# Turning the cross-attention probabilities and the gated mix by transposing DMAs in a one-core hybrid decoder layer

## The chip, the cores and the metric

One core of a Trainium2 chip runs the whole layer. The metric is the device time of one execution in microseconds.

## The reference

One decoder layer over 4096 tokens of width 1024, x <- x + W_out(concat(branch * silu(gate))), all in float32. One input projection of RMSNorm(x) feeds three groups of branches:

```python
proj = rmsnorm(x, norm_g) @ w_in          # 1024 -> 3072
# 8 heads x 64: stick-breaking attention (causal, QK-norm)
sb_out = stick_breaking_attention(q, k, v)
# 4 blocks x 64: width-4 causal convolution, then a gated linear recurrence
lru_out = rg_lru(causal_depthwise_conv(lru_x), ...)
# 4 heads x 64: cross-attention into 256 memory tokens
p = softmax(rmsnorm(xq) @ rmsnorm(mk).T * 64 ** -0.5)
xa_out = p @ mv
y = concat([sb_out * silu(g1), lru_out * silu(g2), xa_out * silu(g3)])
return x + y @ w_out
```

## The kernel before

The 4096 tokens are 32 tiles of 128. Every engine runs the same software pipeline by hand: `body(n, p)` (p is n mod 2) works on tile n in stage A (input projection), tile n-1 in stage B (the branches), tile n-2 in stage C (output projection), and prepares x of tile n+1 in stage X. `steps` runs n = -1 to 1 unrolled, n = 2 to 29 in a loop of 14 pairs, and n = 30 to 33 unrolled. Each engine's program order is fixed by hand; `have(engine, signal, tile)` makes an engine wait until a semaphore says that a step was done for that tile. Every DMA of the loop is issued from SP's queue, in program order; a wait on SP holds back all that is behind it.

Precise products are made of two f16 halves, high and low: x_hi, x_lo for the input, y_hi, y_lo for the mix, `turned[:, 0]` and `turned[:, 1]` for attention weights. `pair_product` (L1285) does hi*hi, hi*lo, lo*hi for 8 blocks of 128 rows, 24 matmuls of 512 columns into one PSUM bank. There are six for the input projection (`project(0)` to `project(5)`) and two for the output.

**TensorE's order in one `body`** (L1293 to L1470): transposes of q, k, cross-attention q and the recurrence's input of tile n-1 (L1309, L1334); project 0; stick-breaking scores (L1350); project 1, project 2; cross-attention scores (L1368) and recurrence gates (L1377); eight f32 transposes of the gated mix `xy` of tile n-2 into the two TURN banks (L1388); project 3; eight transposes of the stick-breaking weights `take` (L1406) into the same banks; project 4; weights times values (L1430, bank HEADS); project 5; a small product that spreads the row scales of the next x (L1412); eight f32 transposes of the cross-attention probabilities `probs` (L1397, in `turn_weights`), again into TURN; output product 0 of tile n-2; probabilities times memory values (L1460 to L1462) and two transposes of the recurrence's result (L1465), which signal `mixed`; output product 1 of tile n-2.

**ACT and DVE around them.** Whatever TensorE turned is taken out of PSUM in halves: ACT writes the high half in f16 (L592 in `turned_high`, L671 for the mix), DVE the low half as value minus high half (L928 in `turned_low`, L1056 for the mix), two instructions of 512 elements each. ACT writes `probs` by exp (L686), the gate sigmoid (L717), the values' high half (L730), x_hi (L738). DVE gates the branches into `xy` (L1138 to L1141), takes the row maximum (L1150), reduces it to a power of two (L1153 to L1159), scales `xy` by it (L1161), and adds the output products to the residual (L1131, L1164). Its first step of the next `body` is the evacuation of the turned q (L956).

**SP's order in one `body`** (L388 to L430): load x for the residual (L394); keep q, k and the attention carry in DRAM (L386); load x for tile n+1 (L405, after the transposes L1388, since they read `xy`) and its turned copy (L407); keep the gate and the values (L386), two copies of the values between partitions (L424, L425); store the output (L428) and wait until it has landed.

`squares`, a scratch for sums of squares, lies on `turned[:, 0]`. `spare` holds weights at the start, later x_res and the recurrence's state; its first 2048 columns are unused in the loop.

Of the kernel before, what the change touches and what calls it, by code (L numbers as in the profile page):

```python
# [27 lines left out]
F16 = mybir.dt.float16  # L28
# [8 lines left out]
P = 128  # L37
# [11 lines left out]
def hybrid_layer(nc, x, x_turned, mem, w_in_g, w_out_g, w_kv_v, per_partition, gate_blocks, out):  # L49
# [35 lines left out]
    with ctx:  # L85
# [11 lines left out]
        def few(n):  # L97
# [46 lines left out]
        mv_raw = [rec_g[:, :, :].rearrange("p h t -> p (h t)"), in_g[:, :, :].rearrange("p h t -> p (h t)")]  # L144
        h_sb = spare[:, KD * GC - D - LW:KD * GC - D].rearrange("p (h t) -> p h t", t=P)
# [49 lines left out]
        y_inv = few(1)  # L195
        y_un = sb("y_un", [P, 2, OC])
# [27 lines left out]
            gate_x gate_l gate_sb xa_scores mx_done neg_done p_done turned_p p_act p_dve  # L224
            conv gates_done gates_read tanh_done beta_steps ui_done beta_done u_done h_done
            mixed rden_done gx_done y_mixed y_steps y_scaled turned_y y_hi_done y_lo_done
# [5 lines left out]

        x_loaded = sem("x_loaded")
# [62 lines left out]
        def have_dma(eng, signal, tile):  # L296

            have(eng, signal, tile, 16)

# [59 lines left out]
        def _(sp):  # L359
# [27 lines left out]

            def body(n, p):  # L388
                X, A, B, C = stages(n)
                q = 1 - p  # L390
                if C:
                    if isinstance(n, int) and n == 2:
                        sp.wait_ge(w_lo, CH)
                    sp.dma_start(x_res, x_t[n - 2]).then_inc(res_loaded, 16)  # L394
                if B:
                    have_dma(sp, kept["q"], n - 2)
                    have_dma(sp, kept["k"], n - 2)
                    keep("q", q_kept, q_t[:, :, :], n - 1, [s["q_evac"]])
                    keep("k", k_kept, k_t[:, q, :, HALF:], n - 1, [s["k_evac"]])
                    have_dma(sp, kept["carry"], n - 2)  # L400
                    keep("carry", carry_kept, carry[:, q, :], n - 1, [s["w"]])
                if X and not (isinstance(n, int) and n < 0):
                    have(sp, s["turned_y"], n - 2)
                    have(sp, s["x_sq"], n)
                    sp.dma_start(xy[:, :], x_t[n + 1]).then_inc(x_loaded, 16)  # L405
                    have(sp, s["x_lo_done"], n)
                    sp.dma_start(x_t32[:, :, :], x_turned[n + 1]).then_inc(xt_loaded, 16)  # L407
                if isinstance(n, int) and n == 0:
                    for c in range(4, CH):
                        load_chunk(c)  # L410
                    sp.wait_ge(seen_made, 1)
                    sp.dma_start(seen[HALF:P, :], seen[0:HALF, :]).then_inc(seen_copied, 16)
                    sp.dma_start(restart[HALF:P, :], restart[0:HALF, :]).then_inc(restart_copied, 16)
                if A:
                    have_dma(sp, kept["gate"], n - 1)
                    have_dma(sp, kept["v"], n - 1)
                    keep("gate", gate_kept, gate[:, p, 0:GC], n, [s["gate_sb"]])
                    keep("v", v_kept, v_sb[:, p, :, :], n, [s["v_read"]])
                    if isinstance(n, int) and n == 0:
                        sp.wait_ge(fail_ones, 1)  # L420
                    have(sp, s["heads"], n - 1)
                    have_dma(sp, v_back_old, n - 1)
                    have_dma(sp, v_back_new, n - 1)
                    sp.dma_start(v_back[HALF:P, p, :, :], v_sb[0:HALF, p, :, :]).then_inc(v_back_old, 16)  # L424
                    sp.dma_start(v_back[0:HALF, q, :, :], v_sb[HALF:P, p, :, :]).then_inc(v_back_new, 16)  # L425
                if C:
                    have(sp, s["out_ready"], n - 2)
                    sp.dma_start(out_t[n - 2], x_res).then_inc(stored, 16)  # L428
                    have_dma(sp, stored, n - 2)
# [109 lines left out]
        def _(act):  # L539
# [56 lines left out]
            def body(n, p):  # L596
# [71 lines left out]
                if C:  # L668
                    have(act, s["turned_y"], n - 2)
                    for b in range(2):  # L670
                        last = act.activation(y_hi[:, 4 * b:4 * b + 4, :], TURN[b][:, :].rearrange("p (k t) -> p k t", t=P),  # L671
                                              ACT.Copy)
                    last.then_inc(s["y_hi_done"], 1)
                if B:
                    have(act, s["gates_read"], n - 1)
                    if isinstance(n, int) and n == 1:
                        act.wait_ge(lam_done, 1)
                    for h in range(LH):
                        act.activation(tanh_l[:, h, :], rec_g[:, h, :], ACT.Tanh, scale=rate[:, h:h + 1])
                        last = act.activation(decay[:, h, :], rec_g[:, h, :], ACT.Exp, scale=rate[:, h:h + 1])  # L680
                    last.then_inc(s["tanh_done"], 1)

                    have(act, s["neg_done"], n - 1)
                    have(act, s["rden_done"], n - 2)
                    for h in range(HX):
                        last = act.activation(probs[:, h, :], SCORE[h % 2][:, (h // 2) * NM:(h // 2 + 1) * NM], ACT.Exp,  # L686
                                              bias=neg_mx[:, h:h + 1], scale=ZSCALE, accum_out=den[:, h:h + 1])
                    last.then_inc(s["p_done"], 1)
# [32 lines left out]
                if isinstance(n, int) and n == 1:  # L721
                    chunk_high(7)
                if A:
# [7 lines left out]
                if B:  # L731
                    have(act, s["turned_p"], n - 1)
                    turned_high(s["p_act"])
                if X:
                    have(act, s["x_scaled"], n + 1)
                    if A:
                        have(act, proj_done[5], n)
                    act.activation(x_hi[:, :, :], x_t32[:, :, :], ACT.Copy).then_inc(s["x_hi_done"], 1)  # L738
                if first:
                    chunk_high(6)  # L740
# [31 lines left out]
        def _(dve):  # L772
# [160 lines left out]
            def body(n, p):  # L933
# [119 lines left out]
                if C:  # L1053
                    have(dve, s["y_hi_done"], n - 2)
                    for b in range(2):
                        last = dve.tensor_tensor(y_lo[:, 4 * b:4 * b + 4, :], TURN[b][:, :].rearrange("p (k t) -> p k t", t=P),  # L1056
                                                 y_hi[:, 4 * b:4 * b + 4, :], ALU.subtract)
                    last.then_inc(s["y_lo_done"], 1)
# [46 lines left out]
                if B:  # L1105
# [5 lines left out]
                                             ALU.mult, ALU.mult).then_inc(s["gx_done"], 1)  # L1111
                if A:
# [3 lines left out]
                if B:  # L1116
                    have(dve, s["p_act"], n - 1)
                    turned_low(s["p_dve"])
# [28 lines left out]
                if B:  # L1147
# [13 lines left out]
                    dve.tensor_scalar(xy[:, :], xy[:, :], y_inv[:, :], TOP, ALU.mult, ALU.mult).then_inc(s["y_scaled"], 1)  # L1161
                if C:
                    have(dve, out_done[1], n - 2)
                    dve.scalar_tensor_tensor(x_res[:, GC:D], PROJ[1][:, :], y_un[:, p, 1:2], x_res[:, GC:D],  # L1164
                                             ALU.mult, ALU.add).then_inc(s["out_ready"], 1)

# [77 lines left out]
        def _(pe):  # L1244
# [48 lines left out]
            def body(n, p):  # L1293
# [25 lines left out]
                if B:  # L1319
# [5 lines left out]
                    have(pe, s["p_act"], n - 2)  # L1325
                    have(pe, s["p_dve"], n - 2)
# [52 lines left out]
                if C:  # L1379
                    have(pe, s["y_scaled"], n - 2)  # L1380
                    if B:
                        have(pe, s["q_evac"], n - 1)
                        have(pe, s["k_evac"], n - 1)
                    else:
                        have(pe, s["p_act"], n - 2)
                        have(pe, s["p_dve"], n - 2)
                    for k in range(KD):
                        last = pe.transpose(TURN[k // 4][:, (k % 4) * P:(k % 4 + 1) * P], xy[:, k * P:(k + 1) * P], ident[:, :])  # L1388
                    last.then_inc(s["turned_y"], 1)
# [4 lines left out]
                def turn_weights(src, signal):  # L1394

                    for i in range(8):
                        last = pe.transpose(TURN[i // 4][:, (i % 4) * P:(i % 4 + 1) * P],  # L1397
                                            src[:, i // 2, (i % 2) * P:(i % 2 + 1) * P], ident[:, :])
                    last.then_inc(signal, 1)

                if B:
                    have(pe, s["w"], n - 1)
                    if C:
                        have(pe, s["y_lo_done"], n - 2)
# [34 lines left out]
                if B:  # L1439
                    have(pe, s["p_done"], n - 1)  # L1440
                    turn_weights(probs, s["turned_p"])
                if C:
                    have(pe, s["y_hi_done"], n - 2)
                    have(pe, s["y_lo_done"], n - 2)
# [3 lines left out]
                if B:  # L1448
                    have(pe, s["p_act"], n - 1)
                    have(pe, s["p_dve"], n - 1)  # L1450
# [111 lines left out]
```

## Time and profile before

| | us |
|---|---|
| median of 3 runs | 1756.45 (1755.13 to 1756.46) |
| the profiled execution: time | 1755.22 |
| the profiled execution: span | 1753.5 |
| TensorE busy in the span | 1672.4 (95%) |
| DVE, ACT, POOL busy | 1062.6, 824.5, 238.3 |

The span runs from the first to the last instruction. A matmul's own duration overlaps that of the next, so two things are read for TensorE: the chain of waits, which gives each group the time that it adds, and idle time before a group. A timeline row is start, busy time, engine, line, operation, output tile <- input tiles, shape, count, and in brackets the idle time before it with what ended it. PE is TensorE, PEld its weight load, SPq the SP queue's issuing instructions. DMA rows give the time from issue until the data has landed. Buffer names are those of the memory's owner: `fail_and_take` holds `take`, `probs` and `v_back`; `spare` holds x_res; `bank` is any PSUM bank.

### The profile page before, as it was taken

What the parts mean: (1) busy time and instruction counts of PE and PEld (TensorE: products, weight loads), DVE (VectorE), ACT (ScalarE), POOL (GpSimd) and SP (SyncE); (2) the same over time, 40 slices, a digit from 0 to 9 for tenths busy, and PEclk for the clock granted to TensorE, in tenths of its full rate; (3) what the DMA queues carried; (4) which work ended last, traced back from release to release, by engine and by line L of the source; (5) the groups of instructions that cost most, each with busy time, mean ns of one, the idle gap of its engine ahead of it and who ended that gap; (6) DMA issues with size and microseconds to landing.
All of it is one profiled execution on the core that took longest, in us unless ns stands there. A gap on an engine that the chain in (4) does not pass through costs nothing.

```text
span 1753.5 us, 29956 instructions
## 1 busy us (share of the span) xinstructions
PE 1672.4 (95%) x11334; PEld 892.9 (51%) x11334; DVE 1062.6 (61%) x2012; ACT 824.5 (47%) x1583; POOL 238.3 (14%) x245
## 2 busy tenths in 40 slices
PE   3886999999999999999999999999999999999986
PEld 1443555555555555555555555555555555555553
DVE  5875655655665565566556556655665665566563
ACT  5844454434545443354554335455433445543441
POOL 0110111110111111011111101111110111111010
PEclk9987999999999999999999999999999999999998
DMA  9411121221211122121112212121221212122111
GB/s 368 146 55 43 54 68 66 72 77 55 78 54 66 66 72 78 54 78 54 66 66 72 78 54 78 54 66 66 72 78 54 78 54 66 66 72 79 55 55 37
DMA packets 61215, 130.03 MB, mean 74 GB/s; under 512 B 10176, under 2 KB 26880, under 8 KB 60032
## 3 DMA queue, kind: packets, MB, share of 16 engines
q1 hardware_dynamic: 60896, 129.49, 21.6%
q8 instruction: 18, 0.29, 0.1%
q10 hardware_dynamic: 288, 0.13, 0.0%
q14 instruction: 13, 0.11, 0.0%
HBM read 70.60 MB, written 50.53 MB: 69 GB/s over the span
## 4 chain that ended last, share of the span: by engine, by line
PE 88%; issue 5%; DVE 3%; ACT 2%; DMA 1%; POOL 1%; POOLq 0%; DVEq 0%; ACTq 0%
PE bank L1288 24%; PE bank L1289 24%; PE bank L1290 24%; PE bank L1309 2%; PE bank L1377 2%; PE bank L1350 2%; PE bank L1368 2%; PE bank L1430 2%; PE bank L1406 2%; PE bank L1397 2%; PE bank L1388 1%; DVE w_pair L859 1%; DMA ident<-ident_flat 1%; PE bank L1412 0%; PE bank L1465 0%
## 5 line engine op out<-in xcount | busy, mean ns | idle before, releaser
L1288 PE MATMUL bank<-w_pair,x_hi 128*128 128x512 f16 x1536 | 587.0, 382 | 5.0 <-DVE w_pair L859 5.0
L1289 PE MATMUL bank<-w_pair,x_hi 128*128 128x512 f16 x1536 | 585.7, 381 | 0.0
L1290 PE MATMUL bank<-w_pair,x_lo 128*128 128x512 f16 x1536 | 585.4, 381 | 0.0
L1290 PEld LDWEIGHTS bank<-w_pair,x_lo 128*128 128x128 f16 x1536 | 151.1, 98 | 184.0 <-issue 4.8
L1288 PEld LDWEIGHTS bank<-w_pair,x_hi 128*128 128x128 f16 x1536 | 151.0, 98 | 176.3 <-issue 14.5
L1289 PEld LDWEIGHTS bank<-w_pair,x_hi 128*128 128x128 f16 x1536 | 151.2, 98 | 165.6 <-issue 3.6
L982 DVE TENSOR_REDUCE ss<-turned 128x8 f32<-128x512 f32 (+1 forms) x96 | 57.4, 598 | 260.2 <-ACT turned L638 172.6
L1288 PE MATMUL bank<-wo_pair,y_hi 128*128 128x512 f16 x512 | 195.3, 381 | 2.6 <-DVE y_lo L1056 2.6
L1289 PE MATMUL bank<-wo_pair,y_hi 128*128 128x512 f16 x512 | 194.9, 381 | 0.0
L1290 PE MATMUL bank<-wo_pair,y_lo 128*128 128x512 f16 x512 | 194.8, 380 | 0.0
L494 POOL TENSOR_TENSOR fail_and_take<-fail_and_take,seen 128x512 f32<-128x512 f32 x32 | 40.5, 1265 | 819.7 <-ACT fail_and_take L631 819.7
L611 ACT ACTIVATE k_t<-bank,given 128x256 f32<-128x256 f32 x32 | 15.1, 473 | 251.5 <-PE bank L1334 251.5
L1017 DVE SCALAR_TENSOR_TENSOR gate<-bank,unscale,gate 128x256 f32<-128x256 f32 (+1 forms) x96 | 54.7, 570 | 118.5 <-ACT gate L717 75.7
L503 POOL TENSOR_TENSOR rs<-rs,columns 128x20 f32<-128x20 f32 x32 | 113.0, 3533 | 5.5 <-POOL rs L501 5.1
L928 DVE SCALAR_TENSOR_TENSOR turned<-bank,turned 128x512 f16<-128x512 f32 x128 | 82.5, 686 | 46.6 <-ACT turned L592 46.6
L616 ACT ACTIVATE q_raw<-bank,unscale 128x512 f32<-128x512 f32 x32 | 22.0, 686 | 128.4 <-PE bank L1290 128.4
L730 ACT ACTIVATE v_sb<-bank 128x512 f16<-128x512 f32 x32 | 19.1, 597 | 134.1 <-PE bank L1290 134.1
L1290 PEld LDWEIGHTS bank<-wo_pair,y_lo 128*128 128x128 f16 x512 | 50.3, 98 | 61.2 <-issue 1.4
L592 ACT ACTIVATE turned<-bank 128x512 f16<-128x512 f32 x128 | 69.1, 594 | 24.6 <-PE bank L1397 24.5
L1288 PEld LDWEIGHTS bank<-wo_pair,y_hi 128*128 128x128 f16 x512 | 50.3, 98 | 56.3 <-issue 3.6
L1289 PEld LDWEIGHTS bank<-wo_pair,y_hi 128*128 128x128 f16 x512 | 50.3, 98 | 54.2 <-issue 0.8
L992 DVE TENSOR_TENSOR_SCAN fail_and_take<-fail_and_take,restart 128x516 f32<-128x516 f32 x64 | 75.1, 1215 | 1.5 <-POOL fail_and_take L494 1.5
(214 smaller groups left out, 2569.1 us busy)
## 6 DMA issues: line engine op xcount, KB each, us to landing
xy<-in_x SPq DMA_DIRECT2D x32, 512.0 KB, 3.3
x_t<-in_x_turned SPq DMA_DIRECT2D x32, 512.0 KB, 4.1
spare<-in_x SPq DMA_DIRECT2D x32, 512.0 KB, 3.8
out<-spare SPq DMA_DIRECT2D x32, 512.0 KB, 2.6
wo_pair<-in_w_in SPq DMA_DIRECT2D x4, 2048.0 KB, 10.1
gate_kept<-gate SPq DMA_DIRECT2D x32, 256.0 KB, 2.0
v_kept<-v_sb SPq DMA_DIRECT2D x32, 256.0 KB, 2.0
fail_and_take<-v_sb SPq DMA_DIRECT2D x64, 128.0 KB, 2.3
```

Of the source, the lines that this page charges most:

```text
L494: pool.tensor_tensor(take[:, :, HALF:], take[:, :, HALF:], seen[:, :].unsqueeze(1).to_broadcast([P, HS, HALF]), ALU.mult).then_inc(s["mask ...
L503: pool.tensor_tensor(rs[:, :], rs[:, :], mhalf_c[:, :].to_broadcast([P, 20]), ALU.pow).then_inc(s["rs_done"], 1)
L592: last = act.activation(turned[:, 0, 4 * b:4 * b + 4, :], TURN[b][:, :].rearrange("p (c t) -> p c t", t=P), ACT.Copy, scale=WTOP)
L928: last = dve.scalar_tensor_tensor(turned[:, 1, 4 * b:4 * b + 4, :], TURN[b][:, :].rearrange("p (c t) -> p c t", t=P), WTOP, turned[:, 0, 4 ...
L982: dve.tensor_reduce(ss[:, at:at + heads], squares[:, 0:heads * HD].rearrange("p (h d) -> p h d", d=HD), AX.X, ALU.add).then_inc(done, 1)
L992: last = dve.tensor_tensor_scan(flat, flat, restart[:, ::-1], 1.0, ALU.mult, ALU.max)
L1017: dve.scalar_tensor_tensor(gate[:, p, cols], src, unscale[:, group:group + 1], gate[:, p, cols], ALU.mult, ALU.mult).then_inc(done, 1)
L1288: pe.matmul(dst, hi[:, k, :], pair[:, 0, k, :], start=k == 0, stop=False)
L1289: pe.matmul(dst, hi[:, k, :], pair[:, 1, k, :], start=False, stop=False)
L1290: last = pe.matmul(dst, lo[:, k, :], pair[:, 0, k, :], start=False, stop=k == KD - 1)
L1309: pe.transpose(dst, src, ident[:, :])
L1350: last = pe.matmul(SCORE[odd][top:top + HALF, c * HW:(c + 1) * HW], q_t[r, c, top:top + HALF], k_t[r, q, c, top:top + HW], start=True, sto ...
```

## The change

Both splits move ahead of the transposes. ACT makes the high half of `probs` (times 2^14) and of `xy` (times its row factor) in f16 in the rows where they lie, in `spare`; DVE makes the low halves. SP then issues four DMAs an iteration with `transpose=True`, each 128 partitions by 1024 f16 elements: two into `turned`, two into `y_hi` and `y_lo`. TensorE's 16 f32 transposes, the evacuations from PSUM and DVE's scaling of `xy` go. TensorE waits for the DMAs instead (`have_turned` is `have` with 32 counts a tile, the 16 of each of two DMAs). The turns of the mix stand first in SP's `body`, those of the probabilities between keeping the gate and keeping the values. Loading x for tile n+1 waits for the low half instead of L1388. ACT now ends its `body` with the mix's high half, DVE with its low half.

```diff
+        p_halves = spare[:, 0:D].bitcast(F16).rearrange("p (a c) -> p a c", a=2)
+        y_halves = spare[:, D:2 * D].bitcast(F16).rearrange("p (a c) -> p a c", a=2)
...
@@ sync @@
+            def turn(dst, src, signal):
+
+                sp.dma_start(dst[:, :, :], src, transpose=True).then_inc(signal, 16)
+
             def body(n, p):
...
                 if C:
+                    have(sp, s["y_low"], n - 2)
+                    have(sp, out_done[1], n - 3)
+                    turn(y_hi, y_halves[:, 0, :], y_turned)
+                    turn(y_lo, y_halves[:, 1, :], y_turned)
...
-                    have(sp, s["turned_y"], n - 2)
+                    have(sp, s["y_low"], n - 2)
                     have(sp, s["x_sq"], n)
                     sp.dma_start(xy[:, :], x_t[n + 1]).then_inc(x_loaded, 16)
...
                 if A:
                     have_dma(sp, kept["gate"], n - 1)
+                    keep("gate", gate_kept, gate[:, p, 0:GC], n, [s["gate_sb"]])
+                if B:
+                    have(sp, s["heads"], n - 1)
+                    have(sp, s["p_low"], n - 1)
+                    turn(turned[:, 0], p_halves[:, 0, :], p_turned)
+                    turn(turned[:, 1], p_halves[:, 1, :], p_turned)
+                if A:
                     have_dma(sp, kept["v"], n - 1)
-                    keep("gate", gate_kept, gate[:, p, 0:GC], n, [s["gate_sb"]])
                     keep("v", v_kept, v_sb[:, p, :, :], n, [s["v_read"]])
@@ scalar @@
-                if C:
-                    have(act, s["turned_y"], n - 2)
-                    for b in range(2):
-                        last = act.activation(y_hi[:, 4 * b:4 * b + 4, :], TURN[b][:, :].rearrange("p (k t) -> p k t", t=P),
-                                              ACT.Copy)
-                    last.then_inc(s["y_hi_done"], 1)
-                if B:
                     have(act, s["gates_read"], n - 1)
...
+                    have(act, s["p_low"], n - 2)
                     for h in range(HX):
                         last = act.activation(probs[:, h, :], SCORE[h % 2][:, (h // 2) * NM:(h // 2 + 1) * NM], ACT.Exp,
...
+                if B:
+                    have(act, s["p_done"], n - 1)
+                    have_turned(act, p_turned, n - 2)
+                    act.activation(p_halves[:, 0, :], probs[:, :, :].rearrange("p h m -> p (h m)"), ACT.Copy, scale=WTOP
+                                   ).then_inc(s["p_high"], 1)
                 if A:
                     have(act, proj_done[5], n)
...
-                if B:
-                    have(act, s["turned_p"], n - 1)
-                    turned_high(s["p_act"])
                 if X:
...
                     act.activation(x_hi[:, :, :], x_t32[:, :, :], ACT.Copy).then_inc(s["x_hi_done"], 1)
+                if B:
+                    have(act, s["y_factor"], n - 1)
+                    have_turned(act, y_turned, n - 2)
+                    act.activation(y_halves[:, 0, :], xy[:, :], ACT.Copy, scale=y_top[:, :]).then_inc(s["y_high"], 1)
@@ vector @@
-                if C:
-                    have(dve, s["y_hi_done"], n - 2)
-                    for b in range(2):
-                        last = dve.tensor_tensor(y_lo[:, 4 * b:4 * b + 4, :], TURN[b][:, :].rearrange("p (k t) -> p k t", t=P),
-                                                 y_hi[:, 4 * b:4 * b + 4, :], ALU.subtract)
-                    last.then_inc(s["y_lo_done"], 1)
...
                                              ALU.mult, ALU.mult).then_inc(s["gx_done"], 1)
+                    have(dve, s["p_high"], n - 1)
+                    dve.scalar_tensor_tensor(p_halves[:, 1, :], probs[:, :, :].rearrange("p h m -> p (h m)"), WTOP,
+                                             p_halves[:, 0, :], ALU.mult, ALU.subtract).then_inc(s["p_low"], 1)
...
-                if B:
-                    have(dve, s["p_act"], n - 1)
-                    turned_low(s["p_dve"])
...
-                    dve.tensor_scalar(xy[:, :], xy[:, :], y_inv[:, :], TOP, ALU.mult, ALU.mult).then_inc(s["y_scaled"], 1)
+                    have(dve, s["y_high"], n - 2)
+                    dve.tensor_scalar(y_top[:, :], y_inv[:, :], TOP, None, ALU.mult).then_inc(s["y_factor"], 1)
                 if C:
                     have(dve, out_done[1], n - 2)
...
+                if B:
+                    have(dve, s["y_high"], n - 1)
+                    have(dve, s["y_factor"], n - 1)
+                    dve.scalar_tensor_tensor(y_halves[:, 1, :], xy[:, :], y_top[:, :], y_halves[:, 0, :],
+                                             ALU.mult, ALU.subtract).then_inc(s["y_low"], 1)
@@ tensor @@
-                if C:
-                    have(pe, s["y_scaled"], n - 2)
...
-                    for k in range(KD):
-                        last = pe.transpose(TURN[k // 4][:, (k % 4) * P:(k % 4 + 1) * P], xy[:, k * P:(k + 1) * P], ident[:, :])
-                    last.then_inc(s["turned_y"], 1)
...
-                if B:
-                    have(pe, s["p_done"], n - 1)
-                    turn_weights(probs, s["turned_p"])
                 if C:
-                    have(pe, s["y_hi_done"], n - 2)
-                    have(pe, s["y_lo_done"], n - 2)
+                    have_turned(pe, y_turned, n - 2)
                     if A:
                         have(pe, s["gate_sb"], n)
                     pair_product(PROJ[0][:, :], y_hi, y_lo, wo_pair[:, 0], out_done[0])
                 if B:
-                    have(pe, s["p_act"], n - 1)
-                    have(pe, s["p_dve"], n - 1)
+                    have_turned(pe, p_turned, n - 1)
                     have(pe, s["gates_read"], n - 1)
```

## Rows read from the trace of the kernel before

**Rows 1.** The page: busy time of each engine, and the chain by engine.
```profile
PE 1672.4 (95%) x11334; PEld 892.9 (51%) x11334; DVE 1062.6 (61%) x2012; ACT 824.5 (47%) x1583; POOL 238.3 (14%) x245
...
PE 88%; issue 5%; DVE 3%; ACT 2%; DMA 1%; POOL 1%; POOLq 0%; DVEq 0%; ACTq 0%
```

**Rows 2.** The chain of one loop iteration: start us, us of the chain, what.
```profile
798.41 0.87 PE bank L1388 x8
...
810.71 0.95 PE bank L1430 x48
...
817.17 0.87 PE bank L1397 x8
...
835.84 1.03 PE bank L1350 x32
...
849.50 0.87 PE bank L1388 x8
```

**Rows 3.** Timeline of PE, same iteration: start us, us busy, line, tiles.
```profile
823.06 0.19 PE L1460 MATMUL bank<-mv_pair,turned 128*128 128x64 f16 x1
```

**Rows 4.** Timeline of ACT, same iteration; in brackets the idle time before.
```profile
799.47 1.10 ACT L671 ACTIVATE y_hi<-bank 128x512 f16<-128x512 f32 x2
800.42 0.44 ACT L679 ACTIVATE tanh_l<-rec_g,columns 128x128 f32<-128x128 f32 x1
...
808.02 1.07 ACT L592 ACTIVATE turned<-bank 128x512 f16<-128x512 f32 x2
...
812.14 0.69 ACT L717 ACTIVATE gate<-bank,unscale 128x512 f32<-128x512 f32 x1
```

**Rows 5.** Timeline of DVE, same iteration.
```profile
809.13 1.29 DVE L928 SCALAR_TENSOR_TENSOR turned<-bank,turned 128x512 f16<-128x512 f32 x2 [0.49 <-ACT turned L592]
...
814.68 0.48 DVE L1110 SCALAR_TENSOR_TENSOR gate<-gate,columns 128x256 f32<-128x256 f32 x1
...
829.39 0.75 DVE L1164 SCALAR_TENSOR_TENSOR spare<-bank,y_un,spare 128x512 f32<-128x512 f32 x1 [0.70 <-PE bank L1290]
830.79 0.75 DVE L956 TENSOR_SCALAR q_t<-bank,given 128x512 f32<-128x512 f32 x1 [0.65 <-PE bank L1334]
```

**Rows 6.** DVE and ACT groups by form: count | busy us, mean ns | idle before.
```profile
L1123 DVE TENSOR_TENSOR x_lo<-x_t,x_hi 128x1024 f16<-128x1024 f32 x32 | 39.2, 1225 | 35.0 <-ACT x_hi L738 35.0
...
L738 ACT ACTIVATE x_hi<-x_t 128x1024 f16<-128x1024 f32 x32 | 33.8, 1056 | 84.2 <-DVE x_t L1010 84.2
```

**Rows 7.** DMA issues: KB each, median us from issue to landing.
```profile
gate_kept<-gate SPq DMA_DIRECT2D x32, 256.0 KB, 2.0
...
fail_and_take<-v_sb SPq DMA_DIRECT2D x64, 128.0 KB, 2.3
...
k_kept<-k_t SPq DMA_DIRECT2D x32, 256.0 KB, 4.1
...
restart<-restart SPq DMA_DIRECT2D x1, 64.5 KB, 7.6
```

**Rows 8.** Timeline of the SP queue, same iteration: the issuing instructions.
```profile
819.85 0.58 SPq L425 DMA_DIRECT2D fail_and_take<-v_sb  x1
830.30 0.34 SPq L428 DMA_DIRECT2D out<-spare  x1
```

**Rows 9.** Windows: busy us of each engine, granted clock, DMA share, GB/s.
```profile
129.00:160.00 31.00, 18.79 (x145) 10.63 (x142) 18.09 (x29) 18.80 (x30) 2.84 (x5) 0.79 0.13 43
...
236.00:1696.00 1460.00, 1454.57 (x10074) 776.12 (x10073) 882.07 (x1629) 679.98 (x1347) 205.98 (x200) 1.00 0.20 66
```

**Rows 10.** The chain in iteration 1.
```profile
153.31 1.72 PE bank L1397 x8
```

**Rows 11.** The drain: DVE timeline, then PE timeline, then SP timeline.
```profile
1731.40 0.75 DVE L1164 SCALAR_TENSOR_TENSOR spare<-bank,y_un,spare 128x512 f32<-128x512 f32 x1 [1.02 <-PE bank L1290]
...
1734.83 0.59 PE L1288 MATMUL bank<-wo_pair,y_hi 128*128 128x512 f16 x1 [2.59 <-DVE y_lo L1056]
...
1734.81 0.34 SPq L394 DMA_DIRECT2D spare<-in_x  x1
```

More of the change, by code:

```diff
@@ L195, in hybrid_layer @@
         y_inv = few(1)
+        y_top = few(1)
         y_un = sb("y_un", [P, 2, OC])
@@ L223, in hybrid_layer @@
             q_read k_read xa_read lru_read sg_read v_hi v_read q_sum k_sum xq_sum rs_mid rs_done normed
-            gate_x gate_l gate_sb xa_scores mx_done neg_done p_done turned_p p_act p_dve
+            gate_x gate_l gate_sb xa_scores mx_done neg_done p_done p_high p_low
             conv gates_done gates_read tanh_done beta_steps ui_done beta_done u_done h_done
-            mixed rden_done gx_done y_mixed y_steps y_scaled turned_y y_hi_done y_lo_done
+            mixed rden_done gx_done y_mixed y_steps y_factor y_high y_low
             x_sq x_rs_mid x_rs x_diag x_wide x_scaled x_hi_done x_lo_done out_ready left_done
@@ L231, in hybrid_layer @@
         out_done = [sem(f"out_done{c}") for c in range(OC)]
+        p_turned = sem("p_turned")
+        y_turned = sem("y_turned")
         x_loaded = sem("x_loaded")
@@ L298, in have_dma, with have_turned @@
             have(eng, signal, tile, 16)
+        def have_turned(eng, signal, tile):
+            have(eng, signal, tile, 32)
         def stages(n):
@@ L722, in body @@
                     chunk_high(7)
+                    act.wait_ge(w_lo, CH)
+                if B:
[3 more added lines that the diff above has]
+                                   ).then_inc(s["p_high"], 1)
                 if A:
@@ L1324, in body @@
                     have(pe, s["y_mixed"], n - 2)
-                    have(pe, s["p_act"], n - 2)
-                    have(pe, s["p_dve"], n - 2)
                     for c in range(4):
@@ L1378, in body @@
                     last.then_inc(s["gates_done"], 1)
-                if C:
-                    have(pe, s["y_scaled"], n - 2)
-                    if B:
[L1382 to L1386, printed above, removed]
-                    for k in range(KD):
-                        last = pe.transpose(TURN[k // 4][:, (k % 4) * P:(k % 4 + 1) * P], xy[:, k * P:(k + 1) * P], ident[:, :])
-                    last.then_inc(s["turned_y"], 1)
                 project(3, [(s["k_read"], n)])
@@ L1393, in body @@
                     chunk_wide(5)
[L1394 to L1399, printed above, removed]
                 if B:
                     have(pe, s["w"], n - 1)
-                    if C:
-                        have(pe, s["y_lo_done"], n - 2)
                     for h in range(HS):
@@ L1438, in body @@
                     memory_keys_turn()
-                if B:
-                    have(pe, s["p_done"], n - 1)
-                    turn_weights(probs, s["turned_p"])
                 if C:
-                    have(pe, s["y_hi_done"], n - 2)
-                    have(pe, s["y_lo_done"], n - 2)
+                    have_turned(pe, y_turned, n - 2)
                     if A:
```

## The prediction

> **What bounds the kernel now.** I read four views in this order: the busy times and the chain by engine, the windows, the chain of one loop iteration, and the timelines of that iteration. TensorE is busy for 95% of the span and holds 88% of the chain [rows 1]. From 236 to 1696 us it is busy for 1454.57 of 1460 us at a granted clock of 1.00 [rows 9]: the loop has no hole in TensorE worth naming. The eight transposes of the gated mix (L1388) start at 798.41 in the chain and again at 849.50 [rows 2], so one iteration takes 51.09 us, and what counts in it is TensorE's own work. DVE and ACT are busy for 882.07 and 679.98 us of the same stretch [rows 9]; they matter only where something on TensorE waits for one of their results.
>
> I take the iteration from 798 to 850 us as the pattern. Its sum is against the profiled execution, 1755.22 us around a span of 1753.5; the median of the runs is 1756.45, 1.2 us above, and I carry the difference over to the median. About 0.2% (3.5 us) is what a measurement can tell from no change.
>
> **Transposes removed.** Both groups of eight lie whole on the chain: 0.87 us for L1388 and 0.87 us for L1397 [rows 2]. That is 1.74 us an iteration. It holds in iterations 2 to 31, 30 of them: 30 x 1.74 = 52.2 us, if nothing takes their place. The period would then be 49.35 us.
>
> **Do the other chains follow?** The next thing on TensorE is the product of the weights with the values (L1430). It starts at 810.71 [rows 2], and the low halves that it needs end on DVE at 809.13 + 1.29 = 810.42 [rows 5]. So it is already tight, and TensorE arriving 0.87 us earlier would gain nothing if DVE did not come earlier too. It does: ACT, which feeds DVE there, loses the evacuation L671, which starts at 799.47, at the head of ACT's unbroken run up to L592 at 808.02; the step behind it starts at 800.42 [rows 4], so without it everything there moves up by 0.95 us. Cost 0; cover gone, it would be 0.87 us an iteration (a rival below).
>
> **The split of the probabilities.** Exact new durations are not in the trace; the nearest forms are 1024 elements from SBUF to f16, 1056 ns on ACT and 1225 ns on DVE [rows 6]. They replace pairs of 512 from PSUM, about 1.07 and 1.29 us [rows 4, 5], so neither engine gets more work, and DVE also loses a scaling of 1024 elements. Bounds: 0.2 us less to 0.5 us more each; no effect on the sum while the slack below holds. ACT: the gate sigmoid ends at 812.14 + 0.69 = 812.83 [rows 4], less 0.95 is 811.9, and the new high half ends at 812.95. DVE: the gating L1110 ends at 815.16 [rows 5], less 0.95 is 814.2, so the low half lasts until about 815.45. The high half is 1.3 us ahead and makes no wait. Behind the low half on DVE stand the value split and the scaling of the next x; they come up to 1.2 us later, but DVE no longer waits there for a second evacuation (1.29), so they are about level.
>
> **The transposing DMAs of the probabilities.** SP waits for the weighted values (done at about 811.7 less 0.9) and for the low half, 815.45. From the end of a DVE result to SP's issue is 830.30 - 830.14 = 0.16 us [rows 5, 8]. One issue occupies SP for up to 0.58 us [rows 8]. A plain DMA lands 2.0 to 4.1 us after its issue for 256 KB, which is this size, and in 2.3 us for 128 KB from SBUF to SBUF [rows 7]. How long a transposing one takes the trace does not show. Low bound: as a plain one, 815.6 + 0.35 + 2.0 = 818.0. Value taken: the second issued 0.6 us after the first, landing by the slow row of 4.1: 815.6 + 0.6 + 4.1 = 820.3. High bound: the copy of a small mask from SBUF to SBUF in 7.6 us [rows 7], though behind the loads of the start, taken one after the other: 815.6 + 15.2 = 830.8. I take the value near the plain rows because a loop transfer of the same size and queue is a nearer neighbour than one copy from the crowded start. TensorE wants the turned halves when it starts L1460, at 823.06 [rows 3] less 1.74 = 821.3. **The slack is 1.0 us by the value taken**, 3.3 by the low bound, and minus 9.5 by the high one. Break-even is where the wait eats 1.74 us: both turns landed 7.6 us after the low half. Order on SP: keeping the gate now stands ahead of the turns (gate ready at 813), keeping and moving the values behind them; those are wanted an iteration later.
>
> The Trainium skill (DMA: Bandwidth & Descriptors, "Latency and other measured facts") gives a transposing DMA 261 GB/s with a non-contiguous middle dimension. By that each 256 KB takes 1.0 us on top of a fixed part, the turns would be landed by about 820, and the forecast would be the same. The same skill has a rule that speaks against the change, told with the rival.
>
> **The transposing DMAs of the mix.** Their splits are at the end of an iteration and TensorE reads them after the middle of the next. The DVE step ahead, L1164, ends at 830.14 [rows 5]; the low half adds 1.2 us to DVE before q's evacuation, L956 at 830.79 [rows 5], which then comes some 0.7 us late against TensorE's faster pace. Who waits: the scores, L1350, at 835.84 [rows 2]; L956 ends 4.3 us before that. Cost 0. SP first waits for the stored output, then issues two turns at about 834, against a use at 817.17 + 51: over 30 us of cover. They stand ahead of reloading x for the output and of keeping q and k, all with an iteration's slack. Loading the next x no longer waits for L1388, so it comes earlier. POOL's queue is not touched. Cost 0, and nothing even at the high bound.
>
> **Start and drain.** In iteration 1 the eight transposes take 1.72 us [rows 10] at a lower clock (mean 0.79 from 129 to 160 us [rows 9]), inside a chain of ACT and DVE steps; I give 1 us back, between 0 and 3. In the last iteration but one, transposes and an evacuation disappear from a loose chain: 2 us back, 0 to 4. In the last one nothing covers the mix: before, the product starts 1734.83 after y_lo [rows 11]. After, DVE's L1164, at 1731.40 + 0.75 [rows 11], comes first, then SP stores and waits until that has landed (its next issue is at 1734.81 [rows 11]), and only then turns: 0.6 + 4.1 more gives 1739.5, 4.7 us later than before. With the plain low bound it is 2.3, with the high one 15. I take 5. Start and drain together: 1 + 2 - 5 = -2.
>
> **Sum.** 52.2 - 2 = 50 us less: 1756.45 - 50 = 1706.
>
> **Rivals.**
> *A, the turned probabilities come too late (slower).* Place: TensorE before L1460, every iteration. For it: the price of a transposing DMA is not in the trace, there are two in a row, the slack is 1.0 us, and nothing else can be done by TensorE while it waits. Against: all rows of this size and queue in the loop. Price by the high bound: 9.5 us of wait. After a wait of that kind TensorE also runs slower for a while: in iteration 1, behind waits, eight transposes take 1.72 instead of 0.87 us [rows 2, 10]; say 2 us more in all. 31 x (9.5 + 2 - 1.74) = +303, and -2 - 10 of start and drain as above: about 2070. It decides from a landing 7.6 us behind the low half. The Trainium skill (VectorE: DVE Perf Modes, "The three transpose paths") has 1309 ns for one 128x128 block by DMA. By that rule, if the eight blocks of a turn do not overlap, one turn is 10.5 us and two are 21, an estimate worse than the high bound; no run here shows it. Chance 0.22 for everything beyond break-even.
> *B, the same wait, but short.* The turns land between 5.9 and 7.6 us behind the low half, and the wait eats part of the gain: with 0.9 us a time, 1706 + 28 = 1734. Chance 0.12, of which 0.02 within 0.2%.
> *C, the weights' chain does not follow.* L1430 waits for DVE as before because ACT is held by something else, and 0.87 us an iteration is lost: 1706 + 27 = 1733. Against: the run on ACT has no gap that a removed L671 would not close. Chance 0.05.
> That the change does not do what it says is not open: both groups of transposes leave TensorE's program, and nothing else of it does.
>
> **How the numbers follow.** Forecast 0.61, A 0.22, B 0.12, C 0.05. Faster: 0.61 + 0.10 + 0.05 = 0.76, same 0.02, slower 0.22. Range of the likeliest case alone: 1698 (start and drain give 5 us back, no cost at the end, a few more tenths an iteration because the value product's tightness loosens) to 1715. To hold 0.8 it must take in C and B up to a wait of 1.3 us: 1698 to 1748. What is left out is A.
>
> **What the changed profile would show.** Right: L1388 and L1397 are gone from TensorE's rows, the iteration takes 49.3 us, the granted clock stays 1.00 from 236 us on, no idle time ahead of L1460's successor, and transposing DMAs land within 4 us. Wrong: an idle time before the product of the probabilities in each iteration with a DMA as releaser (A or B, by its length), or before the value product with DVE as releaser (C). SP's instructions themselves taking microseconds would point to the issue rather than the movement as the cause of A.

## The result and the profile after

The changed kernel takes 1707.41 us (median of 4 runs, 1707.14 to 1708.2) against 1755.79 us for the kernel before on the same chip: ratio 0.9726, 95% interval 0.9709 to 0.9742. That is 48.4 us less; 50 were forecast. The profiled execution has a span of 1705.8 us.

The page of the changed kernel, busy times, DMA and the chain by engine:

```profile
PE 1617.3 (95%) x10822; PEld 836.1 (49%) x10822; DVE 1037.3 (61%) x1948; ACT 828.6 (49%) x1519; POOL 238.1 (14%) x245
...
DMA packets 196382, 163.58 MB, mean 96 GB/s; under 512 B 145344, under 2 KB 162048, under 8 KB 195200
...
q1 hardware_dynamic: 196064, 163.06, 33.3%
...
PE 89%; issue 4%; DVE 2%; ACT 1%; POOL 1%; DMA 0%; SPq 0%; POOLq 0%; ACTq 0%; DVEq 0%
```

TensorE has 512 matmuls fewer (32 tiles by 16 transposes) and is busy 55.1 us less [rows 1]; its share of the span is the same. DVE is busy 25.3 us less, ACT 4.1 us more. The DMA engines carry 33.55 MB more (163.58 against 130.03) in 135,000 more packets, all of them under 512 B, and still stand idle for two thirds of the time.

The chain of one iteration (start us, us of the chain, what); L1414 spreads the row scales of x, L1462 turns the recurrence's result, L1432 is the weights times the values (L1430 before), L1312 a matmul of the projections or of the output:

```profile
794.94 0.22 PE bank L1414 x2
...
801.04 0.25 PE bank L1462 x2
...
837.85 0.24 issue
838.10 0.95 PE bank L1432 x48
839.04 0.32 PE bank L1312
844.33 0.22 PE bank L1414 x2
```

From L1414 to L1414 it is 49.39 us, 1.70 less than the 51.09 of before [rows 2]. Thirty of them make 51.0 us. By the medians, then, start and drain took back 2.6 us, where 2 were forecast. The line "issue" ahead of L1432 is a wait: DVE's low half of the weights ends at 836.50 + 1.29 = 837.79, TensorE is ready at 837.85 and starts at 838.10.

```profile
836.50 1.29 DVE L952 SCALAR_TENSOR_TENSOR turned<-bank,turned 128x512 f16<-128x512 f32 x2 [0.49 <-ACT turned L615]
```

The chain of the kernel before has the same wait at 810.52, 0.19 us. It grew by 0.05 us, about what the loop lacks of the 1.74 of the transposes.

Now the path that could have spoiled it: the DVE timeline, PE's product of the probabilities, and the SP queue. They show two neighbouring iterations: the PE row belongs to the turns at 794.39, the DVE row to the one at 843.77.

```profile
842.45 1.21 DVE L1131 SCALAR_TENSOR_TENSOR spare<-fail_and_take,spare 128x1024 f16<-128x1024 f32 x1
```
```profile
800.18 0.19 PE L1457 MATMUL bank<-mv_pair,turned 128*128 128x64 f16 x1
```
```profile
794.39 2.65 SPq L399 DMA_TRANSPOSE turned<-spare  x2
...
810.28 1.25 SPq L399 DMA_TRANSPOSE y_hi<-spare  x1
811.57 1.33 SPq L399 DMA_TRANSPOSE y_lo<-spare  x1
813.12 0.41 SPq L411 DMA_DIRECT2D spare<-in_x  x1
...
826.44 0.35 SPq L424 DMA_DIRECT2D x_t<-in_x_turned  x1
...
843.77 1.27 SPq L399 DMA_TRANSPOSE turned<-spare  x1
```

DVE's low half ends at 843.66 and SP issues 0.11 us later. One turn holds SP for 1.3 us, against 0.34 to 0.58 for the plain DMAs of [rows 8] (0.64 is the longest plain one of this stretch, the keeping of k). The times to landing are in the DMA view:

```profile
turned<-spare SPq DMA_TRANSPOSE x64, 3.2
...
y_hi<-spare SPq DMA_TRANSPOSE x32, 3.2
y_lo<-spare SPq DMA_TRANSPOSE x32, 3.1
```

The second turn of the pair at 794.39 is issued at 794.39 + 1.34 = 795.73 and lands at 798.93; TensorE comes for it at 800.18. The slack is 1.25 us.

The drain, PE and then SP; before, the same product came after 2.59 us of waiting [rows 11]:

```profile
1686.06 0.61 PE L1312 MATMUL bank<-wo_pair,y_hi 128*128 128x512 f16 x1 [7.92 <-DMA y_lo<-spare]
```
```profile
1678.96 0.34 SPq L451 DMA_DIRECT2D out<-spare  x1
1681.59 1.23 SPq L399 DMA_TRANSPOSE y_hi<-spare  x1
1682.86 1.33 SPq L399 DMA_TRANSPOSE y_lo<-spare  x1
```

### The profile page after: what moved, and what is told of

It is laid out like the page before. It is cut to its first block, busy times and chain, and to the rows that moved or that the text cites. A ratio compares the mean times of both kernels' runs of the same rounds, so it can differ in the third digit from the quotient of the medians.

```text
span 1705.8 us, 29126 instructions
## 1 busy us (share of the span) xinstructions
PE 1617.3 (95%) x10822; PEld 836.1 (49%) x10822; DVE 1037.3 (61%) x1948; ACT 828.6 (49%) x1519; POOL 238.1 (14%) x245
## 2 busy tenths in 40 slices
DMA packets 196382, 163.58 MB, mean 96 GB/s; under 512 B 145344, under 2 KB 162048, under 8 KB 195200
## 4 chain that ended last, share of the span: by engine, by line
PE 89%; issue 4%; DVE 2%; ACT 1%; POOL 1%; DMA 0%; SPq 0%; POOLq 0%; ACTq 0%; DVEq 0%
PE bank L1312 25%; PE bank L1313 25%; PE bank L1314 25%; PE bank L1333 2%; PE bank L1399 2%; PE bank L1390 2%; PE bank L1372 2%; PE bank L1432 2%; PE bank L1408 2%; DVE w_pair L883 1%; PE bank L1462 0%; PE bank L1457 0%; PE bank L1459 0%; PE bank L1458 0%; PE bank L1356 0%
## 5 line engine op out<-in xcount | busy, mean ns | idle before, releaser
L1312 PE MATMUL bank<-w_pair,x_hi 128*128 128x512 f16 x1536 | 587.0, 382 | 5.0 <-DVE w_pair L883 5.0
L1312 PEld LDWEIGHTS bank<-w_pair,x_hi 128*128 128x128 f16 x1536 | 151.2, 98 | 176.5 <-issue 14.5
L1312 PE MATMUL bank<-wo_pair,y_hi 128*128 128x512 f16 x512 | 196.0, 383 | 7.9 <-DMA y_lo<-spare 7.9
L762 ACT ACTIVATE spare<-xy,columns 128x1024 f16<-128x1024 f32 x32 | 36.7, 1147 | 214.2 <-DVE columns L1180 214.2
L1080 DVE TENSOR_TENSOR q_raw<-q_raw,rs 128x512 f32<-128x512 f32 x32 | 37.5, 1173 | 73.2 <-POOL rs L526 73.2
L1312 PEld LDWEIGHTS bank<-wo_pair,y_hi 128*128 128x128 f16 x512 | 50.5, 99 | 62.5 <-DMA y_lo<-spare 8.4
L672 ACT ACTIVATE xq_raw<-bank,unscale 128x256 f32<-128x256 f32 x32 | 15.1, 472 | 121.3 <-PE bank L1314 121.3
```

The lines of the kernel that those rows point to most:

```text
L762: act.activation(y_halves[:, 0, :], xy[:, :], ACT.Copy, scale=y_top[:, :]).then_inc(s["y_high"], 1)
L1080: last = dve.tensor_tensor(raw[:, :, :], raw[:, :, :], rs[:, at:at + heads].unsqueeze(2).to_broadcast([P, heads, HD]), ALU.mult)
L1312: pe.matmul(dst, hi[:, k, :], pair[:, 0, k, :], start=k == 0, stop=False)
```

## The experiments

All ratios are against the kernel before, measured beside each.

**One half of the change alone, twice.** In the first kernel only the mix is split and turned by DMA, in the second only the probabilities. Each is the diff above without the other's lines; on TensorE:

```diff
 e1_mix_only: L1388 goes, L1397 stays
-                        last = pe.transpose(TURN[k // 4][:, (k % 4) * P:(k % 4 + 1) * P], xy[:, k * P:(k + 1) * P], ident[:, :])
+                    have_turned(pe, y_turned, n - 2)
 e2_probs_only: L1397 goes, L1388 stays
-                    turn_weights(probs, s["turned_p"])
+                    have_turned(pe, p_turned, n - 1)
```

> Only the gated mix is split where it lies and turned by DMA; the probabilities go through TensorE as before. My theory (the gain is TensorE's own time for the transposes, 0.87 us a group and iteration, and the DMAs are hidden): 30 x 0.87 = 26 us gained, the drain gives back about 5 (the wait for the DMA in the last iteration, 7.9 us after the change against 2.6 before), so about 1734 us (1730 to 1738), and an iteration of 50.2 us. Rival (the gain comes from lighter ACT and DVE chains or from the earlier load of x, which both belong to the mix): nearly the whole gain is here, about 1710.

> Only the probabilities are split where they lie and turned by DMA; the mix goes through TensorE as before. My theory: 30 x 0.87 = 26 us gained and 1 to 2 in the drain, so about 1728 us (1724 to 1732), if the slack of 1.2 us ahead of the product of the probabilities holds here too; the gate sigmoid on ACT comes 0.95 us later than with both changes while TensorE comes 0.87 us later, so it should. Rival (the gain belongs to the mix): about 1750 or no change.

Measured: the mix alone 1734.7 us, ratio 0.988 (0.9864 to 0.9897); the probabilities alone 1729.4 us, ratio 0.9846 (0.9829 to 0.9862). The gains are 20.4 and 25.6 us, together 46.0, against 48.4 for both at once. The chain of each, mix first, from one product with the values to the next:

```profile
800.24 0.95 PE bank L1430 x48
...
850.52 0.95 PE bank L1430 x48
...
856.97 0.87 PE bank L1399 x8
```
```profile
801.20 0.95 PE bank L1439 x48
...
851.42 0.95 PE bank L1439 x48
```

The first takes 50.28 us, 0.81 less than before; the probabilities' transposes (L1399) are still in its chain. The second takes 50.22 us, 0.87 less. The halves are alike in the loop; the mix alone has the exposed turn of the last iteration. The rival, that the gain belongs to one part's lighter chains, falls.

**The transposes back, without use.**

```diff
+                    for k in range(KD):
+                        pe.transpose(TURN[k // 4][:, (k % 4) * P:(k % 4 + 1) * P], ones[:, :], ident[:, :])
```

once ahead of project 3 and once ahead of output product 0.

> The changed kernel with both groups of eight f32 transposes put back on TensorE at their old places, on a constant, with results that nobody reads; ACT, DVE, SP and the DMAs stay as changed. My theory: TensorE's time alone decides, so about 1707 + 31 x 1.74 = 1761 us (1757 to 1764), at or above the kernel before. Rival (relief of ACT and DVE, earlier loads): part of the gain stays, 1745 or less.

Measured: 1751.58 us (1749.21 to 1752.76), ratio 0.9981 (0.9971 to 0.999). Of the gain of 48, 45 are gone, so TensorE's own time is nearly all of it; but 1751.6 lies below my 1757 to 1764. The chain tells what is left:

```profile
805.28 0.88 PE bank L1438 x48
...
844.00 0.87 PE bank L1406 x8
...
856.10 0.88 PE bank L1438 x48
```

An iteration is 50.82 us, 0.27 less than before, 8 us over the loop, of which start and drain take back more than half (only 3.5 us are left in the medians). Before, the product with the values waited a little for DVE's low half; here the low half ends at 804.36, 0.9 us ahead of the product, the wait of 0.19 is gone and the product itself adds 0.88 instead of 0.95 us. So the rival had a small share: earlier ACT and DVE are worth 0.27 us an iteration when TensorE is not faster. That it is ACT's lost evacuation, and not the other work that left ACT and DVE, was not tried apart. In the changed kernel both come earlier by nearly the same amount, and 0.24 us of wait stays (837.85 above).

**The turned probabilities later.** One more turn of the same size ahead of the two, and SP waits until it has landed:

```diff
                     have(sp, s["p_low"], n - 1)
+                    turn(idle, p_halves[:, 0, :], p_turned)
+                    have(sp, p_turned, n - 1, 48, 32)
                     turn(turned[:, 0], p_halves[:, 0, :], p_turned)
```

> The changed kernel with one more turning DMA of the same size ahead of the two of the probabilities, into unused memory, and SP waiting until it has landed (3.2 us after its issue in the changed kernel's profile, plus a wait of 0.1). My theory: the slack ahead of the product of the probabilities is 1.2 us, so TensorE waits about 2.1 us an iteration: 1707 + 31 x 2.1 + 3 = 1775 us (1765 to 1790), slower than the kernel before. Rival (the turned probabilities are ready long before, so the DMA path does not matter): 1707 to 1712.

Measured: 1774.97 us, ratio 1.0106 (1.0089 to 1.0122): slower than before, and as forecast to the microsecond, but partly by luck: the loop lost less than forecast, start and drain more. Its chain now runs through DVE, the DMA and SP:

```profile
820.40 1.15 DVE spare L1134
821.64 3.08 DMA spare<-spare
824.81 1.23 SPq L400
826.08 3.19 DMA turned<-spare
```

TensorE waits ahead of the product of the probabilities (its row of the PE timeline):

```profile
829.31 0.20 PE L1460 MATMUL bank<-mv_pair,turned 128*128 128x64 f16 x1 [1.73 <-DMA turned<-spare]
```

The iteration is 51.28 us, 1.89 longer (2.1 were forecast), 57 us in thirty iterations; the other 11 us to the changed kernel are start and drain, where 3 were forecast. Against the kernel before, an iteration of the loop is only 0.19 us longer. Of the 20 us between the two, the profiled executions put 5 into iterations 3 to 29 and 15 into the first and the last ones. The granted clock of the loop stayed 1.00 in spite of a wait of 1.7 us in each iteration (windows, 236 to 1650 us):

```profile
236.00:1650.00 1414.00, 1358.92 (x9253) 697.50 (x9251) 831.28 (x1515) 662.51 (x1249) 199.62 (x195) 1.00 0.34 92
```

**One more issue only**, the same edit without the wait.

> As the run with one more turning DMA ahead of those of the probabilities, but SP goes on at once instead of waiting until it has landed. A turn occupies SP for 1.31 us, so the last one lands 1.3 us later. My theory (slack 1.2 us, in which the moves of the three DMAs overlap as two do): a wait of 0.1 to 0.3 us an iteration, 1707 + 31 x 0.2 = 1713 us (1709 to 1717). Rival (turns move one after the other at 3.2 us each, and the profile's landing times hide it): a wait of 2 us, as in the run before, 1770.

Measured: 1715.96 us (1715.54 to 1717.81), ratio 0.9776 (0.9761 to 0.9791). SP's rows:

```profile
847.68 1.27 SPq L400 DMA_TRANSPOSE spare<-spare  x1
849.00 2.71 SPq L400 DMA_TRANSPOSE turned<-spare  x2
```

The last turn is issued at about 850.36 and, 3.2 us later, lands at about 853.56; TensorE's product starts at 853.60. The slack of 1.25 is used up to the last tenth: the iteration is 49.52 us, 0.13 longer, 4 us over the loop. Up to the first tile's second output sum (DVE adds the second output product to the residual) the profiled execution is 2.2 us longer; in that stretch lies a wait of TensorE for the turn in iteration 1, 7.0 us against 5.6 in the changed kernel. Iterations 30 and 32 add 1.7 and 2.3. Turns in a row follow each other at 1.3 us, not at 3.2. Both delays fit a slack of 1.25: 1.3 us later costs 0.13 an iteration, and in the run before, where the two turns were issued 3.2 us later (824.81 against 821.64), it cost 1.89.

**The wait for the stored output moved** from the end of SP's iteration to behind the turns of the mix.

```diff
                     turn(y_lo, y_halves[:, 1, :], y_turned)
+                    have_dma(sp, stored, n - 3)
...
-                    have_dma(sp, stored, n - 2)
...
+            have_dma(sp, stored, NT - 1)
```

> The changed kernel with SP's wait for the stored output moved from the end of its iteration to behind the turns of the mix, right before x is loaded again into the same memory. My theory: nothing in the loop, where the mix has over 30 us of cover, and in the last iteration the turns start 2.6 us earlier: 1704.8 us (1704 to 1706). Rival (the order of SP in the loop matters): a change of 5 us or more either way.

Measured: 1707.65 us (1705.8 to 1708.35), ratio 0.9727 (0.9713 to 0.974). No gain that the runs can tell, and above the range of the forecast. The PE row of the drain shows the wait shorter by 1.4 us, not 2.6, since now the low half itself is the last to come: it ends on DVE at 1682.66 and SP issues the turn at 1682.69. What hides this little is the start: the profiled execution is 2.2 us later than the changed kernel's at the first tile's second output sum (216.10 against 213.88), where the edit has not acted yet. The rival falls: the loop is the same within 0.01 us an iteration.

```profile
1687.25 0.61 PE L1313 MATMUL bank<-wo_pair,y_hi 128*128 128x512 f16 x1 [6.56 <-DMA y_lo<-spare]
```

**The mix turned later**, behind the two loads of x in SP's order.

> The changed kernel with the turns of the mix moved in SP's order from the head of an iteration to behind the two loads of x, which end at 826.8 us in the changed kernel's profile; the turns then land at about 831.4, and the output product reads them at 844.4, so 13 us of cover are left of 32. My theory: no change in the loop, and in the last iteration there are no loads ahead, so 1707 us (1705 to 1710). Rival (SP's order or the bunching of four turns within the second half of an iteration delays the turns of the probabilities): 1712 or more.

Measured: 1710.83 us (1709.57 to 1712.02), ratio 0.9751 (0.9738 to 0.9765), a miss by 1 us at the upper end. The iteration in its chain is 49.39 us as before the edit, so the order in the loop is indeed free. What I had overlooked is the last iteration: the reload of x for the residual now goes ahead of the turns through the same sixteen DMA engines. SP's rows in the loop, and the PE row of the drain:

```profile
827.69 1.28 SPq L399 DMA_TRANSPOSE y_hi<-spare  x1
829.02 2.67 SPq L399 DMA_TRANSPOSE y_lo<-spare  x1
```
```profile
1688.19 0.61 PE L1313 MATMUL bank<-wo_pair,y_hi 128*128 128x512 f16 x1 [9.27 <-DMA y_lo<-spare]
```

The wait is 1.35 us longer than in the changed kernel. Of it 0.47 us are the load issued ahead, and 0.9 the slower landing. Another 1 us of the profiled execution lies ahead of the loop and behind the last sum, and 1 us is between that execution's difference and the median's. Behind 1 MB of loads (L418 and L420, issued at 826.61 and 827.15) the second turn holds SP for 2.67 instead of 1.33 us, and the two land a median of 5.2 and 4.7 us after their issue instead of 3.2 and 3.1.

**A third group by DMA.** The stick-breaking weights are split where they lie, too (from tile 1 on; tile 0 keeps TensorE, since the memory of the halves still holds weights then), in the memory of the probabilities' halves. The scratch for squares of x moves from `turned[:, 0]` to unused memory, and TensorE's eight transposes stay for tile 0 alone, which is why its count of turned tiles is one behind:

```diff
@@ scalar, behind the cross-attention gate @@
+                    act.activation(p_halves[:, 0, :], take[:, :, :].rearrange("p h s -> p (h s)"), ACT.Copy, scale=WTOP
+                                   ).then_inc(s["w_high"], 1)
@@ vector, behind neg_done @@
+                    dve.scalar_tensor_tensor(p_halves[:, 1, :], take[:, :, :].rearrange("p h s -> p (h s)"), WTOP,
+                                             p_halves[:, 0, :], ALU.mult, ALU.subtract).then_inc(s["w_low"], 1)
@@ sync, ahead of keeping the gate @@
+                    turn(turned[:, 0], p_halves[:, 0, :], w_turned)
+                    turn(turned[:, 1], p_halves[:, 1, :], w_turned)
@@ tensor @@
-                if B:
+                if static and n == 1:
                     have(pe, s["w"], n - 1)
                     for h in range(HS):
                         last = pe.transpose(TURN[h // 4][:, (h % 4) * P:(h % 4 + 1) * P], take[:, h, :], ident[:, :])
...
+                    have_turned(pe, w_turned, n - 2)
```

> The changed kernel with the third group of eight f32 transposes, the stick-breaking weights, treated in the same way from tile 1 on: high half by ACT behind the cross-attention gate, low half by DVE behind the cross-attention maxima, two turning DMAs ahead of keeping the gate; the scratch of the squares of x moves to unused memory. My theory (what TensorE does not do is gained as long as the turn has cover; here about 3.4 us): 0.87 us for the transposes and 0.24 us of wait ahead of the product with the values, 30 x 1.11 = 33 us, less 4 in the drain: 1678 us (1672 to 1684). Rival (SP's queue, now with six turns of 1.3 us, or ACT, which is busy without a gap from the gates to the probabilities, becomes the bound, and the probabilities come late): 1695 or more.

> The two kernels before this one together. My theory: the gains add, 1678 - 2.6 = 1675 us (1669 to 1682). Rival as there.

Measured: 1673.41 us (1672.93 to 1674.58), ratio 0.9536 (0.9522 to 0.9551), and with the moved wait 1672.84 us (1671.62 to 1673.41), ratio 0.953 (0.9517 to 0.9543). Both beat the changed kernel by 34 us; the 0.6 us between them are no difference that the runs can tell. The chain, and SP's rows:

```profile
809.63 1.06 PE bank L1408 x8
...
822.14 0.88 PE bank L1452 x48
...
857.83 1.06 PE bank L1408 x8
```
```profile
814.48 2.64 SPq L401 DMA_TRANSPOSE turned<-spare  x2
825.43 0.36 SPq L397 DMA_DIRECT2D gate_kept<-gate  x1
827.97 2.61 SPq L401 DMA_TRANSPOSE turned<-spare  x2
```

48.20 us an iteration, 1.19 less: 0.87 of transposes, 0.24 of the wait ahead of the product with the values, and 0.07 of that product itself, which adds 0.88 instead of 0.95 us to the chain when it doesn't start out of a wait. The weights are turned by about 814.48 + 1.3 + 3.2 = 819.0 and read at 822.14, and the probabilities by 832.5 and read at 833.54: slacks of 3.1 and 1.0 us. Neither SP with six turns nor ACT became the bound.

## Why the prediction was right

*Transposes removed.* Predicted 1.74 us an iteration; the chain lost 1.70, and putting them back took 45 of the 48 us away. Shown. The missing 0.04 is the wait ahead of the product with the values, 0.05 us longer.

*Do the other chains follow.* Predicted: yes, by 0.95 us on ACT. The wait ahead of the product with the values is 0.24 us after and was 0.19 before, so DVE did follow, and rival C did not come. What the prediction did not say is that this wait was a loss already, 0.3 us an iteration with the slower product behind it, that only more relief or another way (the third group) would collect.

*The split.* Predicted from the 1024-element rows: 1.06 and 1.23 us. Measured 1.05 (L744) and 1.21 (L1131) for the probabilities; 1.15 and 1.28 for the mix, whose factor is a column. The low half of the probabilities ended 5.6 us behind the start of the product with the values (843.66 against 838.10), as worked out (815.45 against 810.71 - 0.87).

*The turning DMAs.* This was the open price. I took 0.6 us between the issues and 4.1 to land, 4.7 in all; it is 1.3 and 3.2, 4.5 in all. The sum was right because two errors of 0.7 and 0.9 us cancel: an issue costs SP more than twice a plain one, and the landing is faster than the slow plain row. (Nor was 0.58 the longest plain issue: the same view of before has one of 0.62, the keeping of k.) That is luck, and with a slack this small it mattered: had only the first error been made, the slack would have been 0.3. The slack came out as 1.25 against 1.0.

*Rival A* did not come, but it was near, and the two late runs show that the mechanism and the break-even were as described: at 1.3 us more delay the gain begins to go (0.13 us an iteration), at 3.2 us more it is gone in the loop (1.89 of 1.70), and the kernel is 20 us slower than before, most of it in start and drain. The rule of the Trainium skill named there (VectorE: DVE Perf Modes, "The three transpose paths": 1309 ns for one 128x128 block) can't be summed over blocks: a turn of eight blocks lands in 3.2 us and the next follows at 1.3. The lowered clock that stood in A's price did not show for waits of 1.7 us (granted clock 1.00 in the loop); for 9.5 it was not tried.

*The turns of the mix.* Predicted cost 0 in the loop. Their cover is 30 us (landed at 814.7, read at 844.5); with 18 of them taken away (the run with the mix turned later) nothing changed there. Shown.

*Start and drain.* Predicted 1 + 2 - 5 = -2, measured -2.6 by the medians. The two profiled executions give each term, by the start of the second output sum of each tile (L1164, L1183 after): iteration 1 gave 0.7 us (predicted 1), iterations 2 to 31 gave 51.2 (52.2), the last but one 1.3 (2), the last took 5.8 (5), and 0.2 came behind it, in all 47.7, the difference of the spans. So every term had the right sign and about its size, and each came out a little worse than forecast. The first is not firm: two executions that the edits leave alike up to there lay 2.2 us apart (the run with the moved wait). In the last iteration the wait is 7.92 against 2.59 us, 5.3 more where 4.7 were worked out and 5 taken.

## What to carry to other kernels

Where one engine fills the loop, an operation is worth its own time on that engine, and the question for its replacement is only how long before the reader the data can be ready: write down the producer's end, the issue, the landing and the reader's start, and trust a gain only if all four are in order. A price that the trace lacks is bounded by rows of the same size and queue, and the slack says how wrong it may be. Once the replacement is measured, look for the other places that have the same slack; here the third had more than twice as much and gave 34 us more.

## What was not expected of the hardware

A turning DMA of 128 x 1024 f16 holds SP for 1.23 to 1.35 us, lands 3.2 us after its issue in each of the 64 turns of the probabilities within 0.1, and moves in (196382 - 61215) / 128 = 1056 packets. From the share of the queue, (0.333 x 1705.8 - 0.216 x 1753.5) / 128 = 1.48 us of all sixteen DMA engines for 256 KB, or 177 GB/s, an estimate that puts the whole rise of the queue's share (21.6% before) down to the 128 turns. The Trainium skill (DMA: Bandwidth & Descriptors, "Latency and other measured facts") gives 261 GB/s for a transposing DMA with a non-contiguous middle dimension. This case's share speaks for less, 177 GB/s, which cost nothing here.
